# Splitting weights three units ahead of the matmuls instead of two, in a ring that stays at four units

## What is computed

```python
for layer in range(DEPTH):                       # DEPTH = 2
    if layer % 2 == 0:
        p = x @ w_in                             # 2048 x 6432
        ...                                      # attention on p[:, :3072], rwkv7_group on the rest
        h = jnp.concatenate([o_sb, o_rw], axis=-1).astype(x.dtype) @ ev_w_out[e]
    else:
        h = gated_deltanet(x @ od_w_in[o], od_conv[o], od_a_log[o], od_dt_bias[o],
                           od_norm_w[o]).astype(x.dtype) @ od_w_out[o]
    x = layer_norm(DN_ALPHA * x + h.astype(x.dtype), ln1_g[layer], ln1_b[layer])
    x = layer_norm(DN_ALPHA * x + sq_relu_mlp(x, mlp_w1[layer], mlp_w2[layer]).astype(x.dtype),
                   ln2_g[layer], ln2_b[layer])
```

## Time and profile before

| | |
|---|---|
| median of 3 runs | 3343.9 us (3342.76 to 3344.49) |
| span of the profiled execution, first to last instruction | 3342.8 us |
| TensorE matmuls busy | 3190.1 us (95%) |
| VectorE busy | 1865.1 us (56%) |
| ScalarE busy | 1444.8 us (43%) |
| DMA, mean | 147 GB/s |

### The profile page before, as it was taken

The page is one execution under the profiler, slowest core; times in us unless marked ns, Lnnn a source line. Parts: engine busy times, 40 slices in busy tenths (PEclk is TensorE's granted clock), DMA queues, the critical chain, the costliest instruction groups (busy, mean ns, idle before and its releaser), DMA issues.

```text
span 3342.8 us, 57029 instructions
## 1 busy us (share of the span) xinstructions
PE 3190.1 (95%) x22180; PEld 2942.7 (88%) x22180; DVE 1865.1 (56%) x2397; ACT 1444.8 (43%) x2153; POOL 55.3 (2%) x32
## 2 busy tenths in 40 slices
PE   8999998989999999989999999999999999999997
PEld 7888888879898989889999998899987989999896
DVE  5555555575455554565556556555575654555455
ACT  3443334334343444434445555454454344434442
POOL 1000000010000000010000000000000100000000
PEclk9999999989999999989999999999999899999999
DMA  6233233446555565544333324443334555555553
GB/s 211 88 97 92 87 92 107 140 154 201 191 184 188 188 190 183 191 141 133 102 101 127 110 93 139 139 152 102 101 126 139 170 189 188 187 188 187 190 185 118
DMA packets 157019, 492.36 MB, mean 147 GB/s; under 512 B 15584, under 2 KB 50528, under 8 KB 155792
## 3 DMA queue, kind: packets, MB, share of 16 engines
q1 hardware_dynamic: 154032, 476.18, 44.2%
q0 software_dynamic: 2240, 12.07, 1.0%
q10 hardware_dynamic: 544, 1.05, 0.1%
HBM read 487.14 MB, written 2.10 MB: 146 GB/s over the span
## 4 chain that ended last, share of the span: by engine, by line
PE 82%; DVE 10%; ACT 4%; issue 3%; DVEq 0%; DMA 0%; ACTq 0%; SPq 0%
PE pp L397 67%; DVE wl L1238 3%; PE mb L711 2%; PE mb L725 2%; PE mb L705 2%; DVE ws L1579 1%; ACT wh L809 1%; PE mb L547 1%; PE mb L535 1%; PE mb L737 1%; PE mb L743 1%; PE mb L553 1%; PE mb L505 0%; DVE ws L1663 0%; ACT ws L1106 0%
## 5 line engine op out<-in xcount | busy, mean ns | idle before, releaser
L1238 DVE TENSOR_TENSOR wl<-raw,wh 128x1024 fp32r<-128x1024 f32 (+1 forms) x936 | 1128.9, 1214 | 891.4 <-ACT wh L809 882.8
L809 ACT CAST wh<-raw 128x1024 fp32r<-128x1024 f32 (+1 forms) x936 | 943.6, 1018 | 953.0 <-PE pp L397 952.3
L397 PE MATMUL pp<-aTh,wh 128*128 128x256 f32 x4400 | 1292.5, 294 | 59.4 <-DVE wl L1238 39.1
L397 PE MATMUL pp<-aTl,wh 128*128 128x256 f32 x4400 | 1255.5, 285 | 0.0
L397 PE MATMUL pp<-aTh,wl 128*128 128x256 f32 x4400 | 1255.4, 285 | 0.0
L397 PEld LDWEIGHTS pp<-aTh,wh 128*128 128x128 f32 x4400 | 854.9, 194 | 75.5 <-issue 47.2
L397 PEld LDWEIGHTS pp<-aTl,wh 128*128 128x128 f32 x4400 | 855.3, 194 | 4.6 <-issue 3.9
L397 PEld LDWEIGHTS pp<-aTh,wl 128*128 128x128 f32 x4400 | 853.8, 194 | 0.0
L397 PE MATMUL pp<-wh,hTh 128*128 128x512 f32 x1408 | 560.2, 398 | 17.2 <-DVE hTl L1609 7.8
L397 PE MATMUL pp<-wh,hTl 128*128 128x512 f32 x1408 | 551.1, 391 | 0.0
L397 PE MATMUL pp<-wl,hTh 128*128 128x512 f32 x1408 | 550.8, 391 | 0.0
(11 more groups left out here) (271 smaller groups left out, 2120.1 us busy)
## 6 DMA issues: line engine op xcount, KB each, us to landing
raw<-in_w_dram SPq DMA_DIRECT2D x800, 512.0 KB, 4.2
raw<-in_w_dram SPq DMA_DIRECT2D x136, 384.0 KB, 3.5
ws<-in_ln_dram POOLq DMA_DIRECT2D x8, 1024.0 KB, 9.0
out_dram<-xres SPq DMA_DIRECT2D x8, 256.0 KB, 2.0
ws<-in_lora_dram POOLq DMA_DIRECT2D x8, 192.0 KB, 2.6
xres<-in_x_dram ACTq DMA_DIRECT2D x2, 512.0 KB, 6.1
xres<-in_x_dram SPq DMA_DIRECT2D x2, 512.0 KB, 7.1
ws<-in_c_dram POOLq DMA_DIRECT2D x1, 832.0 KB, 8.1
```

Source lines behind the costliest of these rows:

```text
L397: last = mm(o, lhs, rhs, start=opens and m == 0, stop=end and kk == 1 and m == 2, skip_group_check=True)
L809: nc.scalar.copy(wh[:, q % RING, :, 0:width], raw[:, q, :, 0:width]).then_inc(S("hi_ready"), 1)
L1238: tt(wl[:, q % RING, :, 0:width], raw[:, q, :, 0:width], f(wh[:, q % RING, :, 0:width]), ALU.subtract).then_inc(S("lo_ready"), 1)
```

## The change

One constant. It is read by `interleave` on ScalarE and VectorE (L121, L129, L130) and by the two loops that split the first units of the program (L823, L1259). The ring, the raw buffers, the evacuations and TensorE's order stay.

```diff
@@ -35,7 +35,7 @@
 LNX_EPS = 64e-5
 KK_EPS = 1e-12
 SB_SCALE = 128.0 ** -0.5
-LEAD = 2
+LEAD = 3
```

## The result

The changed kernel takes 3368.7 us (median of 4 runs, 3367.8 to 3372.2), the kernel before on the same chip 3343.3 us (3342.0 to 3344.5). The ratio is 1.008, with a 95% interval of 1.0068 to 1.0091: slower by 25 us, where 19 were forecast. The profiled execution has a span of 3370.5 us; against the 3342.8 us of the earlier trace rows that is +27.7 us.

A forecast was written before the change was run, and what follows sets the result against it. TensorE, busy 95% of a 3342.8 us span, was taken to bound the kernel. The terms -15.9 -3 +4 +17.1 +6 +7 +3.8 summed to +19 us, that is 3363 us, range 3343 to 3384.

The forecast's parts named there:

- The scalings, -15.9 and -3 at the start: Three scalings of x: each regains 2.9 us of pause and 2.4 of half clock, -15.9 us; program start: -3 us.
- Layer 0, +4: Layer-0 groups: 1 us gained in all, half clock behind six merged 2.5 us pauses counted against it; together +4 us.
- I take half: Layer-0 groups: half clock behind the new pauses costs between 0 and 10 us; half of that was taken.
- The layer-1 mixers, 17.1 and 6: Start of eight layer-1 mixers: splits wait one unit later, delaying the sigmoid, +17.1 us; half clock behind new pauses, +6 us.
- nothing after it gives this back: Layer-1 mixers: the delay before L672 stays, as the rest of the group is released by the same chain.
- The tails, 7 and 3.8: Two output tails feeding a layer norm: residual additions behind later splits hold up TensorE, +7 us and +3.8 us.
- the slower one by the clock (3375): Rival, whole kernel: every new pause of 2 us and more is followed by half clock, 3375 us; chance 0.10.
- The chain alone (3351): Rival, whole kernel: losses as in the sum, but no new pause brings the clock down, 3351 us; chance 0.17.
- no change: Rival: scaling gains as forecast, half the loss at the mixers, no new half clock, 3344 us; chance 0.12.
- The faster rival: Layer-1 chain catches up, TensorE waits under 1 us at L672: sum -4, or -34 (3310 us) with more; chance 0.11.
- the case in which all 40.2 us are gained: Part of the faster side: all TensorE waits for the low half go, nothing is lost, 3304 us; chance 0.03.

The follow-up runs named there:

- run 1: Kernel before with lead three only where x is transposed and scaled (first narrow panel, two MLPs, gates stage), lead two elsewhere: 3325.9 us, -16.8 (ratio 0.9946).
- run 11: Changed kernel (lead three everywhere) with GpSimd scaling one element instead of all of x, work left out: 3357.8 us, +13.6 against the kernel before (1.0041).
- run 3: Kernel before with lead three only in the layer-0 groups and the output stage carrying the last layer-0 mixer: 3350.8 us, +8.1 (1.0024).
- run 8: Changed kernel with six small unused matmuls in front of each wait before L493 and L672: 3358.6 us, +15.1 against the kernel before (1.0050).
- run 2: Kernel before with lead three only in the stages with a layer-1 mixer and the one stage between them: 3362.1 us, +19.3 (1.0055).
- run 5: Kernel before, still lead two, with only ScalarE's wait for the ring made one unit stricter: 3370.9 us, +27.3 (1.0084).
- run 6: Kernel before with lead three only from the eleventh of 30 steps in each layer-1 mixer stage, two again at its end: 3333.7 us, -9.9 (0.9973).
- run 4: Kernel before with lead three only in the two output tails that feed a layer norm: 3354.0 us, +11.3 (1.0035).
- run 12: Lead three only in the two output tails, with residual addition and statistics ahead of the split there: 3345.1 us, +1.2 against the kernel before (1.0004).

## Why the prediction was right

The forecast of 3363 us lies 6 us under the median, and each part has its sign. The chains that the sum was built on are in the traces. How often a new pause brings half clock was a guess, and the guess was wrong. By its steps:

*The scalings, -15.9 and -3 at the start.* Run 1 gives -16.8 for both, run 11 -17.7. The pause became 1.42 us (1.5 said), and the clock behind it 1.00, so that the 2.4 us of each came back as counted. The interval of run 1 takes in the -18.9, so the runs do not tell whether too much was claimed.

*Layer 0, +4: mis-sized.* The chain was read rightly: with both low halves there in time TensorE waits 2.90 us for L901 (2.5 said), which ends where its own chain lets it:

```profile
237.82 1.22 PE L493 MATMUL mb<-ws 128*128 128x256 f32 x2 [2.90 <-ACT ws L901]
```

The term that failed is "I take half", for the share of pauses that bring the clock down. All six did. Measured +8.1 in run 3, and run 8 shows that it is all clock. One reading was loose: of the six pairs of waits five are as long as said, and the sixth is 0.77 and 1.23 us.

*The layer-1 mixers, 17.1 and 6: right as a sum, in part by luck.* The delay of the sigmoid was to be 2.57 us and is 2.58, the wait before L672 was to be 2.75 and is 2.75, and all eight were to make about 20 us and make 22.0. Measured +19.3 in run 2 and 21.1 in the stretch. Run 5 shows that the stricter wait for the ring alone delays the mixers, run 6 that the loss sits in the first ten steps. Of the 17.1 us, 15.4 belong to this stretch, which leaves out the first group's 1.7. In the stretch TensorE stands still 10.9 us longer (stretch less busy time: 48.2 us, was 37.3) and is busy 10.1 us longer with the same 6617 matmuls. Run 5 is 13.6 us longer and run 8 10.6, both at 0.99 as before. So the chain costs some 11 to 14 us and not 15.4: "nothing after it gives this back" fails, since of 16.8 us more before L672 3.0 come back at L1649 and the rest in small pieces elsewhere. The clock costs some 7 to 10 us and not 6: seven of the eight pauses were followed by half clock, where half were counted. The two errors go opposite ways.

*The tails, 7 and 3.8.* The stretch before the first layer norm is 9.3 us longer and the one before the third 4.3 us (32.7 where it was 28.4) by the trace; run 4 gives 11.3 for both, and run 12 takes it away by order alone. The addition sits where it was put, behind a split that follows unit 29:

```profile
706.87 1.22 DVE L1284 TENSOR_TENSOR xres<-xres,pp 128x1024 f32<-128x1024 f32 x1
...
708.14 0.50 PE L397 MATMUL pp<-wh,hTh 128*128 128x512 f32 x1 [3.58 <-DVE xres L1284]
...
715.06 1.22 DVE L1284 TENSOR_TENSOR xres<-xres,pp 128x1024 f32<-128x1024 f32 x1
```

The first tail was put at 8.1 with half clock behind both new pauses, and 7 was taken. It came out at 9.3, at a clock of 0.75 over the stretch where it was 0.85: half clock followed both, and cost more than counted.

*The rivals.* Of the four, the slower one by the clock (3375) had the better mechanism: it let half clock follow every new pause of 2 us and more, and in the changed kernel's trace half clock followed all of them but the one of 2.75 us before the sixth L672. Its time is 6 us too long, as the forecast's is 6 us too short: for the mixers alone it has 29 us, and they cost 19 to 21. The forecast took about half of every such term; that this came as near to the time as it did is luck in part. The chain alone (3351) is out, as is no change. The faster rival decides at L672, and there TensorE waits 2.75 us. With it falls the case in which all 40.2 us are gained. The Trainium skill (Perfetto Trace Analysis, Optimization Strategy) says to find the gaps of the engine that one optimizes for and to make the dependency behind them start sooner. Here 30.2 of the 40.2 us left the list, and the kernel became 25 us slower.

## What to carry to other kernels

A deeper lead in a ring of the same size is also a stricter wait, and everything that stands behind that wait on an in-order engine moves with it: before such a change, look in each stage at what comes next in program order, and keep the deep lead for the stages where a known stall needs it (here -17 us there, and +39 us in the other stages). A wait that vanishes from the list is no gain until the next chain has been timed. Placing counts as much as depth: one split moved out of the end of each layer-1 group gave 9 to 10 us, and the addition put ahead of the split gave back the 11 us that the deeper lead had cost in the tails.

## What the runs showed of the hardware

TensorE's clock fell after shorter pauses than I had counted with. Pairs of pauses of 1.39 us and less, some 9 us apart, left it at 1.00 in six groups of the kernel before. In the changed kernel one pause stands in the place of each pair, 2.9 us in five groups and 2.2 us in the sixth, and half clock followed all six, at 1.6 us a group over the five. A pause of 1.4 us behind the scaling left it up. The shortest pause that was followed by half clock in the changed kernel is this one; the stretch behind it has a mean clock of 0.62:

```profile
2062.72 1.15 PE L672 MATMUL mb<-cc,ws 128*128 128x128 f32 x8 [1.88 <-DVE ws L1634]
```

The length alone does not decide in these traces. Two pauses of 2.67 us in the kernel before, which end at 2010.09 and 2449.04 us, were followed once by half clock and once not:

```profile
2010.09:2014.50 4.41, 4.41 (x12) 0.61 0.40 123
2449.04:2453.00 3.96, 3.96 (x17) 1.00 0.31 117
```

The 2.2 us pause was followed by full clock in run 3, and the 1.88 us pause in run 11. Six matmuls whose results are not used, put into the pause, kept the clock up at every L493 and L672 of run 8.

The other surprise is how the same delay is booked: a chain that is late by one unit stood as L1634 before L672 with three units ahead (run 2), and mostly as L1238 before L397 with two (run 5).
